# RWKV projections by Strassen's scheme: seven products of half depth in place of eight, in pairs of projections

## What is computed

```python
xn = rms_norm(h, norm_g)
proj = jnp.concatenate([prev_xn[:, None, :], xn], axis=1) @ w_in
cur = proj[:, 1:, :n_sh]
mixed = cur + (proj[:, :-1, :n_sh] - cur) * mu
mem_q, gate = jnp.split(proj[:, 1:, n_sh:], [W_MEM], axis=-1)
r, k, v, wd, ad, vd = jnp.split(mixed, ...)
decay = jnp.exp(-jnp.exp(log_w))           # log_w from tanh(wd) @ w_up
a = jax.nn.sigmoid((a0 + ad @ a_up))
kk = k * k_k / |k * k_k|
# per token: S_t = S_(t-1) (diag(decay_t) - kk_t^T (kk_t * a_t)) + v_t^T k_t ;  o_t = S_t r_t
y = jnp.concatenate([o, mo], axis=-1) * jax.nn.silu(gate)
```

## Time and profile before

| | |
|---|---|
| time, median of 3 runs | 2050.29 us (2048.61 to 2054.89) |
| the profiled execution's own time | 2057.22 us |
| its span | 2055.3 us |
| PE busy | 1912.8 us (93%) |
| DVE busy | 963.2 us (47%) |
| ACT busy | 635.1 us (31%) |
| POOL busy | 305.1 us (15%) |
| products of the projections (L772), busy | 401.2 us, 1152 records |

### The profile page before, as it was taken

One profiled execution on the slowest core, in us unless ns is written; L12 is line 12 of the kernel. 1 busy time (PEld: TensorE's weight loads), 2 busy tenths in 40 slices (PEclk: granted clock), 3 DMA queues, 4 the chain that ended last, 5 costly groups with the idle time before them and its releaser, 6 DMA issues. The chain is left out here.

```text
span 2055.3 us, 44993 instructions
## 1 busy us (share of the span) xinstructions
PE 1912.8 (93%) x19534; PEld 1314.8 (64%) x19534; DVE 963.2 (47%) x2083; ACT 635.1 (31%) x1499; POOL 305.1 (15%) x286
## 2 busy tenths in 40 slices
PE   6999989999999899897998999999999899799997
PEld 3577575675765757654443699995556566566664
DVE  4354373553734636332323476585233788633332
ACT  6322322222222223121224323232323566511111
POOL 0100030020300302111001010100010566201010
PEclk9999999999999999999999999999999999799998
DMA  8010010010100101007102130210200100667662
GB/s 290 18 37 3 22 34 23 18 39 22 34 23 12 45 22 34 24 17 263 57 1 107 53 116 32 96 52 11 92 22 11 62 1 1 236 201 231 214 223 77
DMA packets 53943, 147.70 MB, mean 72 GB/s; under 512 B 11587, under 2 KB 21123, under 8 KB 52468
## 3 DMA queue, kind: packets, MB, share of 16 engines
q1 hardware_dynamic: 43764, 103.97, 14.9%
q0 software_dynamic: 9984, 40.87, 5.7%
HBM read 123.58 MB, written 21.24 MB: 70 GB/s over the span
## 5 line engine op out<-in xcount | busy, mean ns | idle before, releaser
L772 PE MATMUL psum<-xT,rw_w 128*128 128x384 f32 (+1 forms) x1152 | 401.2, 487 | 0.0
L772 PEld LDWEIGHTS psum<-xT,rw_w 128*128 128x128 f32 x1152 | 205.7, 190 | 115.7 <-issue 10.7
L1368 DVE SCALAR_TENSOR_TENSOR rwkv_xs<-psum,rwkv_pc,rwkv_xsc 128x64 f32<-128x64 f32 x90 | 25.6, 284 | 225.2 <-PE psum L1033 225.2
L740 POOL DMA_DIRECT2D out<-rwkv_s x6 | 5.8, 960 | 638.5 <-ACT rwkv_out_p L1178 638.5
L1156 ACT COPY rwkv_r_sb<-psum 128x64 f32<-128x64 f32 x96 | 20.3, 212 | 258.4 <-PE psum L1003 256.0
L1625 PE MATMUL psum<-xT,gate_w 128*128 128x384 f32 (+1 forms) x288 | 97.3, 488 | 1.9 <-PEq L169 1.9
L1549 PE MATMUL psum<-xT,y_r 128*128 128x512 f32 (+1 forms) x180 | 87.2, 617 | 8.4 <-DMA y_r<-gated 8.4
L2904 PE MATMUL psum<-V,yT 128*128 128x512 f32 x192 | 92.7, 604 | 0.0
L3106 ACT COPY xT<-psum 128x384 f32<-128x384 f32 x64 | 30.5, 476 | 169.1 <-PE psum L3015 169.1
L3140 DVE COPY xT<-psum 128x384 f32<-128x384 f32 x64 | 35.6, 556 | 95.1 <-PE psum L3015 95.0
L919 PE MATMUL psum<-rwkv_dd,rwkv_am 64*64 64x64 f32 x1968 | 67.7, 219 | 9.8 <-issue 9.7
(11 more groups left out here) (514 smaller groups left out, 4136.3 us busy)
## 6 DMA issues: line engine op xcount, KB each, us to landing
kp<-in_cache_k SPq DMA_DIRECT2D x64, 384.0 KB, 4.0
xT<-in_cache_v POOLq DMA_DIRECT2D x48, 384.0 KB, 4.3
rw_w<-in_w_in SPq DMA_DIRECT2D x28, 512.0 KB, 3.6
gate_w<-in_cache_v POOLq DMA_DIRECT2D x16, 384.0 KB, 5.7
front_w<-in_mem_w_kv SPq DMA_DIRECT2D x2, 2048.0 KB, 14.5
x_rows<-in_x_p SPq DMA_DIRECT2D x8, 512.0 KB, 13.9
...
```

The source lines that it names most:

```text
L772: mm = pe.matmul(out, w[:, load % 2, k, :], xT[:, k, a:b], start=(k == 0), stop=(k == KC - 1))
```

## The change

Two projections X = (R, K) are made together by a form of Strassen's scheme for the first two pieces of columns (768 tokens), and Y = (G, V) in the same way. The output is seen as a 2 x 2 grid (projection by piece of columns), the depth as two halves (`KH` = 4 chunks): eight products of half depth become seven, `X0` to `X6`, of sums of weights and sums of activations. The third piece of columns (328) is still made directly: K2, R2, V2, G2.

- The sums of activations (`token_sums`) are made once by DVE: `U2`, `U3` in the new buffer `u_own`, `U4` in `mkT` and `mv`, and one overwrites a quarter of `xT`. What stood there is saved to DRAM by three DMAs first (`lent_d`) and brought back before the last recurrence's fill goes on.
- The sums of weights (`weight_sums`, `first_sum`) are made by DVE for each pair and each of X and Y: `F2`, `F3` in `f_own`, `F4` in the ends of `mkT` and `mv`.
- The products are joined by DVE in SBUF (`joins`, 7 additions for X and 7 for Y); product 0 is copied by ACT (`first_copy`). When they are joined, ACT scales 768 columns and DVE mixes them at once (`scaled_sums`, `mixed_sums`).
- The order of the pieces is new: K2, then X with W and A in between, then R2, V2, H, then Y, then G2. The steps at which the pieces end are so: K2 in 1; X0 in 2; X1 in 3; X2, X3 in 4; X4, W2, A2 in 5; X5 in 6; X6 in 7; R2 in 8; V2 in 9; H in 10; Y0, Y1 in 11; Y2 in 12; Y3, Y4 in 13; Y5 in 14; Y6 in 15; G2 in 16.
- To make room, `arT` has one buffer in place of two (the last chunks of it are written at step 15), `masked` one in place of two (its second half is made at step 6), `out_p` is `rs_sb`, and `keep` is spread over `dinv` by DVE ahead of the scan.

The diff, cut to its core:

```diff
-PIECES = "W0 A0 K0 W1 A1 K1 W2 A2 K2 R0 R1 H0 R2 H1 V0 H2 V1 V2 G0 G1 G2".split()
-PARTS = [(i, k) for i, name in enumerate(PIECES) for k in range(KC if name[0] in "KRVG" else 1)]
+PIECES = ("K2 W0 A0 X0 X1 W1 A1 X2 X3 W2 A2 X4 X5 X6 R2 V2 H0 H1 H2 " + " ".join(f"Y{j}" for j in range(7)) + " G2").split()
+DEPTH_OF = {**{c: KC for c in "KRVG"}, **{c: KC // 2 for c in "XY"}}
+PARTS = [(i, k) for i, name in enumerate(PIECES) for k in range(DEPTH_OF.get(name[0], 1))]
...
+        SIDES = (w[:, 1], w[:, 0])
+
+        def product(kind, j, k):
+            one, two = SIDES
+            x = [[xT[:, half * KH + k, part * CW:(part + 1) * CW] for part in range(2)] for half in range(2)]
+            return ((one[:, k, :], x[0][0]), (F2[:, k, :], U2[:, k, :]), (F3[:, k, :], U3[:, k, :]), (one[:, KH + k, :], x[1][0]),
+                    (two[:, KH + k, :], U4[k // 2][:, k % 2, :]), (two[:, k, :], x[0][1]), (F4[k // 2][:, k % 2, :], x[1][1]))[j]
...
         def _(sp):
+            for d, t in zip(lent_d, lent):
+                sp.dma_start(d, t).then_inc(lent_out, 16)
+            sp.dma_start(lent_d[2].rearrange("p (k c) -> p k c", k=KH), X12).then_inc(lent_out, 16)
...
+                elif kind in "XY":
+                    n, j = 2 * q + "XY".index(kind), int(PIECES[i][1])
+                    if k == 0 and j == 0 and kind == "Y":
+                        pe.wait_ge(w_loaded[1], 16 * (2 * q + 1))
+                    if k == 0 and j == 1:
+                        pe.wait_ge(sums_ready, 1)
+                        pe.wait_ge(factors_ready, n + 1)
+                    if k == 0 and j == 5:
+                        pe.wait_ge(first_ready, n + 1)
+                    left, right = product(kind, j, k)
+                    mm = pe.matmul(out, left, right, start=(k == 0), stop=(k == KH - 1))
...
+            def scaled_sums(q, kind, src, n):
+                act.wait_ge(joined, 14 * q + {"K": 5, "R": 7, "V": 12}[kind])
+                act.wait_ge(mix_read, 6 * q + n - 1)
+                nc.scalar.activation(prev[:, 1:1 + 2 * CW], src[:, 0:2 * CW], ACT.Copy, scale=vec(vecs, "mu", W_CHUNK[kind] + q)).then_inc(prev_ready, 1)
...
+                    elif PIECES[i] == "X5":
+                        scaled_sums(q, "K", kT, 2)
+                    elif PIECES[i] == "X6":
+                        scaled_sums(q, "R", rT, 3)
+                        act.wait_ge(mix_read, 6 * q + 2)
+                        nc.scalar.activation(kkT, kT[:, :], ACT.Square, scale=vec(vecs, "k_k", q)).then_inc(sq_ready, 1)
+                    elif PIECES[i] == "Y5":
+                        scaled_sums(q, "V", vT, 6)
+                    elif PIECES[i] == "Y6":
+                        act.wait_ge(joined, 14 * q + 14)
+                        act.wait_ge(mix_read, 6 * q + 6)
+                        nc.scalar.activation(prev[:, 0:2 * CW], gT[q % 2][:, 0:2 * CW], ACT.Tanh, scale=0.5).then_inc(g_tanh, 1)
...
-                if n == 7:
+                if n == 9:
                     act.wait_ge(cum_ready, q + 1)
...
+                for out, src, after in (((c12, c11, 0),), ((c22, c12, 1),), ((c11, c11, 1),), ((c21, c22, 2),), ((c22, c22, 4), (c12, c12, 4)),
+                                        ((c12, c12, 6),))[j - 1]:
+                    if after:
+                        dve.wait_ge(joined, n + after)
+                    nc.vector.tensor_tensor(out, src, ps, ALU.add).then_inc(joined, 1)
...
+            def weight_sums(q, kind):
+                one, two = SIDES
...
+                link(nc.vector.tensor_tensor(F3, one[:, 0:KH, :], two[:, 0:KH, :], ALU.subtract))
+                link(nc.vector.tensor_tensor(F2, two[:, KH:KC, :], F3, ALU.subtract))
+                for part in range(2):
+                    k = slice(2 * part, 2 * part + 2)
+                    ins = nc.vector.tensor_tensor(F4[part], one[:, KH + 2 * part:KH + 2 * part + 2, :], F2[:, k, :], ALU.subtract)
+                ins.then_inc(factors_ready, 1)
...
+            def token_sums():
+                x11, x21, x22 = xT[:, 0:KH, 0:CW], xT[:, KH:KC, 0:CW], xT[:, KH:KC, CW:2 * CW]
+                link(nc.vector.tensor_tensor(U3, x22, X12, ALU.subtract))
+                link(nc.vector.tensor_tensor(U2, U3, x11, ALU.add))
+                dve.wait_ge(lent_out, 48)
+                nc.vector.tensor_tensor(X12, X12, x11, ALU.subtract)
+                for part in range(2):
+                    k = slice(2 * part, 2 * part + 2)
+                    ins = nc.vector.tensor_tensor(U4[part], x21[:, k, :], U2[:, k, :], ALU.subtract)
+                link(ins)
+                dve.sem_inc(sums_ready, 1)
...
+                if n == 15:
+                    kkc = kkT.rearrange("p (n t) -> p n t", t=CH)
+                    nc.vector.tensor_tensor(ar[:, 11:NPC, 1, :], chunks(rT)[:, 11:NPC, :], dec[:, 11:NPC, 1:CH + 1], ALU.mult)
+                    nc.vector.scalar_tensor_tensor(out=ar[:, NPC - 2:NPC, 0, :], in0=kkc[:, NPC - 2:NPC, :], scalar=-1.0,
+                                                   in1=dec[:, NPC - 2:NPC, 0:CH], op0=ALU.mult, op1=ALU.mult)
+                    nc.vector.tensor_tensor(kaT[:, :], kaT[:, :], dinv[:, :], ALU.mult)
+                    nc.vector.scalar_tensor_tensor(out=beT[:, :], in0=beT[:, :], scalar=0.5, in1=dinv[:, :], op0=ALU.mult,
+                                                   op1=ALU.mult).then_inc(prep_ready, 1)
```

More of the change, by code:

```diff
@@ L79, in make_constants @@
     put("id2", h_ == c64)
[L80 to L83 removed]
+    put("keep", np.broadcast_to(np.arange(HS) > 0, (P, HS)))
     put("ownseq", h_ // TS == np.arange(B)[None, :])
@@ L609, in rwkv_pairs @@
         xsc = st.sb("xsc", [P, HS])
-        r_sb, sa_sb, rs_sb, sas_sb, out_p = [st.sb(n, [P, HS]) for n in ("r_sb", "sa_sb", "rs_sb", "sas_sb", "out_p")]
+        r_sb, sa_sb, rs_sb, sas_sb = [st.sb(n, [P, HS]) for n in ("r_sb", "sa_sb", "rs_sb", "sas_sb")]
+        out_p = rs_sb
         s0 = st.sb("s0", [P, B, HS])
         s1 = st.sb("s1", [P, B, HS])
-        masked = st.sb("masked", [P, 2, B, NS])
+        masked = st.sb("masked", [P, B, NS])
+        u_own = st.sb("u_own", [P, 2, KC // 2, 384])
+        f_own = st.sb("f_own", [P, 2, KC // 2, P])
         expd = st.sb("expd", [P, 2, B, HS])
@@ L954, in sample_part @@
                         for d in half:
-                            mm = pe.matmul(bank[d, 2, 0:HS], masked[d, 0, b, :], s1[d, b, :], start=False, stop=(b == B - 1))
+                            mm = pe.matmul(bank[d, 2, 0:HS], masked[d, b, :], s1[d, b, :], start=False, stop=(b == B - 1))
                     if n == SP_R + 1:
@@ L971, in sample_part @@
                         for d, to in zip(half, other):
-                            mm = pe.matmul(bank[to, 2, 2 * HS:3 * HS], masked[d, 1, b, :], s1[d, b, :], start=False, stop=(b == B - 1))
+                            mm = pe.matmul(bank[to, 2, 2 * HS:3 * HS], masked[d, b, :], s1[d, b, :], start=False, stop=(b == B - 1))
                     if n == SP_O + 1:
@@ L1002, in recurrence @@
                         for d, to in zip(half, other):
[L1003 removed]
+                            mm = pe.matmul(bank[d, 0, 0:HS], arT[d, n, 0, :], x[d, :], start=False, stop=True)
                             if n != 8:
[L1005 removed]
+                                pe.matmul(bank[to, 1, at:at + HS], arT[d, n, 1, :], x[d, :], start=True, stop=False)
                     mm.then_inc(r_mm, 1)
@@ L1026, in recurrence @@
                         for d, to in zip(half, other):
-                            pe.matmul(bank[to, 1, at:at + HS], arT[d, p % 2, n, 1, :], x[d, :], start=True, stop=False)
+                            pe.matmul(bank[to, 1, at:at + HS], arT[d, n, 1, :], x[d, :], start=True, stop=False)
                         for d, to in zip(half, other):
@@ new lines, in weight_sums @@
+            def weight_sums(q, kind):
+                one, two = SIDES
+                n = 2 * q + "XY".index(kind)
+                if n >= 1:
+                    for side in range(2):
+                        dve.wait_ge(w_loaded[side], 16 * n)
+                    dve.wait_ge(piece_done, piece(q, "X6") if kind == "Y" else piece(q - 1, "Y6"))
+                else:
+                    dve.wait_ge(lent_out, 48)
[5 more added lines that the diff above has]
+                ins.then_inc(factors_ready, 1)
@@ L3209, in build @@
         y_d = nc.dram_tensor("gated", (P, KC, TT), F32).ap()
+        lent_d = [nc.dram_tensor(f"lent{n}", (P, width), F32).ap() for n, width in enumerate((1024, 1024, KC // 2 * 384))]
         xT = sb("xT", [P, KC, TX])
```

199 lines of the change are left out of this document (132 added, 67 removed).

## The result

| | before | after |
|---|---|---|
| median of the runs, us | 2050.5 | 2090.6 |
| ratio after / before, 95% interval | | 1.0172 [1.0150, 1.0194] |
| profiled execution, us | 2057.2 | 2094.6 |
| its span, us | 2055.3 | 2092.9 |
| mean granted clock | 0.981 | 0.972 |

A forecast was written before the change was run, and what follows sets the result against it. PE was taken as the bound. Waits of 8.2 against 5.1 gained gave +3.0 us a pair, +15 for five; with +6.3 for the first pair, +21 on 2050.3: 2072 us, range 2046 to 2090.

The forecast's parts named there:

- What is removed: Fill products on PE: 64 of 384 columns become 56, eight fewer at 0.64 each, 5.1 us a pair gained.
- Step 7: From T, the start of `xs` on DVE, `r_sb` waits behind X6's join, scale and square; PE loses 2.5 us.
- The end of the recurrence: ACT's tanh of Y6 waits for the last join, ahead of `o_all`; PE loses 2.5 us in turning v.
- Steps 6, 5, 9, 10, 13 and 14: Smaller PE waits on ACT and DVE: 0.3, 0.1, 1.0, 0.2, and 1.6 for the last two together.
- half clock 1.3: First pair: PE runs at half clock for a while behind 8 us of idling ahead of X1; costs 1.3 us.
- The first pair: No recurrence to hide in: PE idle 8.0, half clock, later waits, less 5.1: +6.3 us, bounds +3 and +12.
- The rule on POOL and DVE: First pair: by SBUF contention the sums of tokens start 2.1 later, end at 86.7, and cost almost nothing.
- The DMAs: Three saves of `xT` ahead of the third sum of tokens land at 85 to 90, 86.5 taken; reload costs nothing.
- 1 (waits covered): ACT and DVE operations overlap more than chained, so the kernel gets faster: 2038, without any waits 2031; chance 0.15.
- 4 (products don't shrink): Pieces of four save nothing, through more starts or weight loading: +46, 2096 us; chance 0.02.
- Rival 3: DVE is late too in steps 5, 9 and 13, waits of 11 to 12: +39, 2089 us; chance 0.15.
- the last part of the prediction: Signs: 2.5 idle at step 8 and at the end, recurrences of 94 to 95 us; otherwise right by accident.

The follow-up runs named there:

- e4: Changed kernel plus PE products nobody reads, filling the waits at step 8 and ahead of `o_all`; nothing moved: ratio 1.0099, 15 us less than the changed kernel.
- e8: Changed kernel with the edits of e2 and e3, and DVE's `prT` and first `arT` operation one step earlier: ratio 0.9967 to the kernel before.
- e1: Changed kernel with ACT's square of k moved from step 7 to the head of step 8: ratio 1.0123, 10 us less than the changed kernel.
- e2: Changed kernel with ACT's scale of R and square of k and DVE's mix of R moved from step 7 to step 8: ratio 1.0044, 26 us less.
- e3: Changed kernel with ACT's tanh of Y6 and DVE's gate product of it moved behind the copy of `o_all`: ratio 1.0110, 13 us less.
- e6: Changed kernel with POOL's memset and fills waiting until the sums of tokens are made; read from the trace: DVE's two sums fall from 2.67 and 2.53 to 1.76.
- e7: Changed kernel with W1 A1 W2 A2 ahead of X1 and, in the first pair, K2 mixed before the sums of weights: ratio 1.0142, 6 us less.

## Why the prediction was right in its sign and 19 us short

- **What is removed** (5.1 us a pair): right. PE is busy 1904.7 us in place of 1912.8, only 8.1 less, but e4's 1911.2 less its five times 2.72 and 2.27 us of filling are 1886.3, 26.5 less than before, with the first pair's lower clock still in it. A recurrence without long waits (e8) takes 83.2 against 86.9 with 1.0 us more idle time in it, so 4.7 us less of work, and part of the last step's saving lies behind its last `r_sb`.
- **Step 7**, 2.5 us: right in size and in mechanism. Forecast were T+2.2, 3.0, 4.1 and 4.4 for the ends of join, scale and square and the restart of PE; measured T+2.2, 3.2, 4.3 and 4.42. e1 and e2 moved its two causes and the wait followed, 1.62 and 0.20.
- **The end of the recurrence**, 2.5: 2.20 measured, with join and copy ending at T+3.75 and T+5.1 as forecast. The semaphore that I added to 2.4 wasn't needed (and the second half of the turning began at T+2.8 before, not T+2.7). e3 took the wait away.
- **Steps 6, 5, 9, 10, 13 and 14**: 3.2 forecast (0.3, 0.1, 1.0, 0.2, 1.6). The waits of PE show 0.24 more behind step 6's feed (0.44 against 0.20), 0.24 behind step 9's (0.45 against 0.21), nothing from 5 and 10, and 0.52 and 0.90 ahead of the last two `sa_sb`: 1.9. Step 9's 1.0 was four times too much; the last two steps were sized well (1.4 against 1.6).
- **The sum of waits** is then 6.6 a pair (2.72 in place of 0.20 in step 8, 2.20, 1.9) and not 8.2, and with the 5.1 saved the pair would have lost 1.5, not the forecast 3.0 (8.2 less 5.1 is 3.1). By the waits alone the prediction was too high.
- **The term that failed is the clock.** "PE is idle 8.0, half clock 1.3" stands in the first pair's sum, from the earlier trace rows, and no such term stands in the hidden pairs, though two waits of over 2 us were forecast in each. The rows show 1.7 us behind step 8 in the third pair (4.17 - 2.47); by the length of the step it is 1.5 to 1.7 in four pairs and 2.8 in the fourth, 9.2 in all. Behind the boundary it is about 1.5 in four of five (1.97 - 1.15, and the decay products at 0.64 instead of 0.38). That is 15 us, and e4 takes it out: 15 us by the runs, 16.8 by the trace, so 3.0 to 3.4 a pair. 5 x (1.5 + 3.0 to 3.4) = 23 to 25 of the 29.3 that the five pairs lost. So the size of the total, as far as it was met, was helped by luck: waits put 1.6 a pair too high against a clock term put at nothing.
- **What is left**, 5 to 7 us in the five stretches between recurrences, is not settled. PE's idle time there is spread over waits of 0.3 to 1.9 us at places that differ from pair to pair, before the change too, and no run singled one out. Much of it may be no more than the difference between two executions: in e6 and e7, whose five stretches hold the same instructions and the same two long waits, they add up to 246.6 and 248.7 us, against 251.1 in the changed kernel's profile, the slowest of its four runs. The 2.2 us behind the last recurrence are no part of the change's work either.
- **The first pair**, +6.3: measured +5.5 (the first `r_sb` comes 108.1 behind the stage's first product, 102.6 before), and this near only because two terms were off against each other. PE was idle 5.97 and not 8.0, since it was done later than forecast (87.7, not 85.1; the stage began 0.7 later, and K2 ran partly at the lower clock, 6.34 in place of 4.65). And the lower clock behind the wait cost 2.6 (5.49 - 2.85), twice the 1.3 taken. Y1 waited 0.54 and the third decay product 0.76, forecast were 0.8 and 1.3.
- **The rule on POOL and DVE**: the prediction cited the Trainium skill (GPSIMD Engine Reference, Specifications) for contention between the two, and by that rule the sums of tokens would start 2.1 later. They started at 81.8, behind a POOL memset of 3.89 (forecast 81.0; the stage itself began 0.7 later), and then took 2.67 and 2.53: DVE lost its time in the sums and not ahead of them. e6 shows that the contention is real, and that it was the longer of the two chains here: with it the third sum started at 87.1, 9.4 behind the stage's first product, without it at 85.9, 7.7 behind it, when the DMAs had landed (86.5 forecast). The prediction had the two chains even.
- **The DMAs** landed at 85.8. The last recurrence lasts 70.5 us in both kernels, and PE has no wait for a DMA in any recurrence, so reload and weights cost nothing that can be seen.
- The rivals: 1 (waits covered) and 4 (products don't shrink) are excluded by the rows above. Rival 3 gave 2089, and its number is the better one, but its cause isn't: the waits were 6.6 and not 11 to 12. By the last part of the prediction, which asked for 2.5 at step 8 and at the end and for recurrences of 94 to 95 us, the first two are there; from window to window the recurrence lasts 96.5, and what it has too much is the clock.
